# The gated activation of the second feed-forward: formed with tokens on the partitions, and only the product transposed

## What is computed

```python
D_FF_2 = -(-8 * D_MODEL // (3 * 256)) * 256
h = rmsnorm(x, norm_ffn[layer])
a, b = jnp.split(h @ w_ffn_in[layer], 2, axis=-1)
x = x + ((jax.nn.silu(a) * b) @ w_ffn_out[layer]).astype(x.dtype)
```

## Time and profile before

| | |
|---|---|
| three executions | 868.4, 869.7, 872.04 us |
| the profiled execution, its own time | 871.05 us |
| its span, first to last instruction | 868.8 us |
| mean granted clock of TensorE | 0.969 of full speed |
| TensorE matmuls, busy | 797.1 us (92%), 3811 instructions |
| VectorE, busy | 550.6 us (63%) |
| ScalarE, busy | 485.9 us (56%) |
| GpSimd, busy | 86.6 us (10%) |
| weights and inputs read | 128.6 MB, 149 GB/s over the span |
| second feed-forward, wide groups and down groups | from 686 to 865 us |

### The profile page before, as it was taken

How to read it: one execution, slowest core, us unless ns; L and a number is a source line. 1 busy time by engine, 2 the same in 40 slices (tenths; PEclk the granted TensorE clock), 3 DMA queues, 4 the chain that set the end, 5 groups by cost and what they waited for, 6 DMA issues and landing times.

```text
span 868.8 us, 10702 instructions
## 1 busy us (share of the span) xinstructions
PE 797.1 (92%) x3811; PEld 647.7 (75%) x3811; DVE 550.6 (63%) x817; ACT 485.9 (56%) x743; POOL 86.6 (10%) x50
## 2 busy tenths in 40 slices
PE   4989999999799999999999798796859999999998
PEld 3777788777588888888887577663637888888886
DVE  5676676567556777776463477687673666665650
ACT  4755656666236777774264744342543677776630
POOL 0023000000000000000000056644231000000000
PEclk9989999999999999999999899798969999999999
DMA  8766333344237655456383533221001675554550
GB/s 303 292 203 198 103 116 119 97 147 140 68 120 251 211 193 193 151 170 204 105 270 124 179 98 97 78 68 49 25 25 48 215 237 182 177 184 173 191 165 24
DMA packets 70566, 130.21 MB, mean 150 GB/s; under 512 B 5534, under 2 KB 17142, under 8 KB 70142
## 3 DMA queue, kind: packets, MB, share of 16 engines
q1 hardware_dynamic: 69662, 124.90, 44.2%
q10 hardware_dynamic: 864, 4.78, 1.5%
HBM read 128.61 MB, written 1.05 MB: 149 GB/s over the span
## 4 chain that ended last, share of the span: by engine, by line
PE 74%; DVE 11%; ACT 7%; DMA 4%; issue 2%; POOL 1%; SPq 1%; ACTq 0%; DVEq 0%; POOLq 0%
PE acc L478 20%; PE acc L480 20%; PE acc L479 20%; DMA b_raw<-in_w_in 2%; DVE b_wlo L1186 2%; PE banks L579 2%; PE banks L704 2%; PE banks L539 2%; PE banks L564 2%; PE banks L717 1%; DMA b_raw<-in_w_mem_kv 1%; ACT b_whi L825 1%; PE banks L552 1%; PE banks L543 1%; PE banks L566 1%
## 5 line engine op out<-in xcount | busy, mean ns | idle before, releaser
L1186 DVE TENSOR_TENSOR b_wlo<-b_raw,b_whi 128x1024 fp32r<-128x1024 f32 (+4 forms) x222 | 253.1, 1179 | 102.8 <-ACT b_whi L825 101.4
L825 ACT ACTIVATE b_whi<-b_raw 128x1024 fp32r<-128x1024 f32 (+4 forms) x244 | 234.3, 1001 | 77.1 <-DMA b_raw<-in_w_in 19.3
L478 PE MATMUL acc<-b_whi,b_hhi 128*128 128x512 f32 (+4 forms) x528 | 205.0, 388 | 10.3 <-DVE b_hlo L1459 4.6
L479 PE MATMUL acc<-b_whi,b_hlo 128*128 128x512 f32 (+4 forms) x528 | 198.2, 375 | 0.0
L480 PE MATMUL acc<-b_wlo,b_hhi 128*128 128x512 f32 (+4 forms) x528 | 197.8, 375 | 0.0
L478 PEld LDWEIGHTS acc<-b_whi,b_hhi 128*128 128x128 f32 x528 | 100.9, 191 | 31.0 <-DVE b_hlo L1459 5.1
L480 PEld LDWEIGHTS acc<-b_wlo,b_hhi 128*128 128x128 f32 x528 | 100.8, 191 | 15.8
L479 PEld LDWEIGHTS acc<-b_whi,b_hlo 128*128 128x128 f32 x528 | 100.8, 191 | 15.8 <-issue 1.5
L478 PE MATMUL acc<-b_whi,b_ohi 128*128 128x512 f32 (+1 forms) x272 | 105.8, 389 | 5.4 <-DVE b_wlo L1186 2.9
L480 PE MATMUL acc<-b_wlo,b_ohi 128*128 128x512 f32 (+1 forms) x272 | 103.4, 380 | 0.0
L479 PE MATMUL acc<-b_whi,b_olo 128*128 128x512 f32 (+1 forms) x272 | 103.1, 379 | 0.0
(11 more groups left out here) (214 smaller groups left out, 909.0 us busy)
## 6 DMA issues: line engine op xcount, KB each, us to landing
b_raw<-in_w_in SPq DMA_DIRECT2D x48, 512.0 KB, 4.8
b_raw<-in_w_ffn_up SPq DMA_DIRECT2D x40, 512.0 KB, 4.8
b_raw<-in_w_ffn_in SPq DMA_DIRECT2D x40, 512.0 KB, 4.7
b_raw<-in_w_ffn_down SPq DMA_DIRECT2D x22, 512.0 KB, 6.0
b_raw<-in_w_ffn_out SPq DMA_DIRECT2D x22, 512.0 KB, 4.7
b_raw<-in_w_out SPq DMA_DIRECT2D x16, 512.0 KB, 3.7
b_raw<-in_w_in SPq DMA_DIRECT2D x12, 412.0 KB, 3.6
b_raw<-in_w_in SPq DMA_DIRECT2D x8, 410.0 KB, 3.5
```

The costliest lines, as they stand in the source:

```text
L478: nc.tensor.matmul(o, a, wh, start=first, stop=False)
L479: nc.tensor.matmul(o, b, wh, start=False, stop=False)
L825: A(whi[:, n % SPLIT, 0:c["nk"], 0:c["n"]], raw[:, n % RAW, 0:c["nk"], 0:c["n"]], ACT.Copy)\
L1186: V.tensor_tensor(wlo[:, n % SPLIT, 0:c["nk"], 0:c["n"]], raw[:, n % RAW, 0:c["nk"], 0:c["n"]], whi[:, n % SPLIT, 0:c["nk"], 0:c["n"]].bit ...
```

## The change

The feed-forward of the second block gets functions of its own, `ffn2`, on TensorE, ScalarE and VectorE; `ffn1` is the old code for the first. In `ffn2` the sums of the gate half are read twice by ScalarE (scaled Copy to `gtok`, scaled Abs to `ltok`); Exp, Ln, the logarithm, Exp and the weighing y * sigmoid follow with tokens on the partitions. VectorE then reads the sums of the up half, multiplies by the token's norm factor and by the weighed gate and writes `utok`. TensorE transposes `utok` alone (banks 0 and 1), ScalarE writes the high part straight from the bank and VectorE the low part. `etok` and `ltok` are other views of the buffers `e` and `lg`.

```diff
+        etok, ltok = [b.rearrange("p c t -> p (c t)").rearrange("p (t n) -> p t n", t=T) for b in (e, lg)]
...
+            def act_T(i=0, short=""):
+                for t in range(T):
+                    pe.wait_ge(*moved(f"u2{short or '_0'}", t, i))
+                for b in range(1 if short else 2):
+                    claim(b, f"a2{short}T", i)
+                    for c in range(2):
+                        for t in range(T):
+                            mm = nc.tensor.transpose(X[b][:, c * S + t * P:c * S + (t + 1) * P],
+                                                     utok[:, t, (2 * b + c) * P:(2 * b + c + 1) * P], ident)
+                    full(mm, b, f"a2{short}T", i)
+
+            def ffn2():
+                after_norm("ffn2", "g2s", "u2s")
+                gemm("g2_0", 0)
+                gemm("g2_0", 1)
+                act_T(short="s")
+
+                with pe.Fori(0, PAIRS - 1) as i:
+                    cnt.enter()
+                    gemm("u2_0", 0, i)
+                    gemm("u2_0", 1, i)
+                    gemm("g2_0", 0, i + 1)
+                    act_T(i)
+                    gemm("g2_0", 1, i + 1)
+                cnt.leave(PAIRS - 1)
+                gemm("u2_0", 0, PAIRS - 1)
+                gemm("u2_0", 1, PAIRS - 1)
+                for c in range(-(-FT // (CK * PART))):
+                    if c < PAIRS:
+                        pe.wait_ge(*at("bank1 free", "a2T", c))
+                    gemm("d2_0", c)
+                    if c == 0:
+                        act_T(PAIRS - 1)
+                gemm("d2_1")
...
+                def gate_in(i=0, short=""):
+                    name, n = f"g2{short or '_0'}", REST if short else CN
+                    if not short:
+                        v = cnt.value("gate weighted", "2", i) - 1
+                        act.wait_ge(sem("gate weighted"), v if known else 1)
+                    for t in range(T):
+                        a = sums(act, name, t, i)
+                        scaled(gtok[:, t, 0:n], a[:, 0:n], ACT.Copy, "ffn2", t)
+                        leave(scaled(ltok[:, t, 0:n], a[:, 0:n], ACT.Abs, "ffn2", t), name, t, i)
...
+                hi_to(first + PART - 1)
+                gate_in(short="s")
+                hi_to(first + 2 * PART - 1)
+                gate_log(short="s")
+                hi_to(first + 3 * PART - 1)
+                sigmoid(short="s")
+                hi_to(first + 4 * PART - 1)
+                act_hi(short="s")
+                with act.Fori(0, PAIRS) as i:
+                    cnt.enter()
+                    gate_in(i)
+                    for n in range(PER, PER + PART):
+                        hi_one(first + n, i)
+                    gate_log(i)
+                    for n in range(PER + PART, PER + 2 * PART):
+                        hi_one(first + n, i)
+                    sigmoid(i)
+                    for n in range(PER + 2 * PART, 2 * PER):
+                        hi_one(first + n, i)
+                    act_hi(i)
...
+                def product(i=0, short=""):
+                    name, n = f"u2{short or '_0'}", REST if short else CN
+                    dve.wait_ge(*at("gate weighted", f"2{short}", i))
...
+                    for t in range(T):
+                        a = sums(dve, name, t, i)
+                        leave(V.scalar_tensor_tensor(utok[:, t, 0:n], a[:, 0:n], rs[:, rstd("ffn2", t)],
+                                                     etok[:, t, 0:n], ALU.mult, ALU.mult), name, t, i)
...
+                with dve.Fori(0, PAIRS) as i:
+                    cnt.enter()
+                    for n in range(PER, PER + PART):
+                        lo_one(first + n, i)
+                    gate_log(i)
+                    for n in range(PER + PART, PER + 2 * PART):
+                        lo_one(first + n, i)
+                    weigh(i)
+                    for n in range(PER + 2 * PART, 2 * PER):
+                        lo_one(first + n, i)
+                    product(i)
+                    act_lo(i)
```

More of the change, by code:

```diff
@@ L946, in gate_in @@
                         blk = FT - 2 if short else 4 * i + 2 * b
[L947 to L955, removed]
+                        for c in range(2):
+                            ins = A(y[:, 2 * b + c, :], X[b][:, c * S:(c + 1) * S], ACT.Identity,
+                                    bias=vT[:, bass.ds(blk + c + 3 * FT, 1)],
+                                    scale=vT[:, bass.ds(blk + c + 2 * FT, 1)])
+                        done(ins, "gate in", f"{m}{short} {b}", i)
                 def finish(i=0, short=""):
@@ L991, in ffn, with ffn2, gate_log, sigmoid @@
                 hi_to(groups[f"d{m}_0"]["last"] + 2 * PART)
[L992 to L995, removed]
+                norm("x2", "d1_1", hhi, None, "norm_ffn_2")
+            def ffn2():
+                first = groups["g2_0"]["first"]
+                def gate_in(i=0, short=""):
[7 more added lines that the diff above has]
+                        leave(scaled(ltok[:, t, 0:n], a[:, 0:n], ACT.Abs, "ffn2", t), name, t, i)
+                def gate_log(i=0, short=""):
+                    n = REST if short else CN
+                    act.wait_ge(*moved(f"g2{short or '_0'}", 1, i))
+                    done(A(ltok[:, :, 0:n], ltok[:, :, 0:n], ACT.Exp, scale=-1.0), "gate exp", f"2{short}", i)
+                    act.wait_ge(*at("gate exp", f"2{short}", i))
+                    done(A(ltok[:, :, 0:n], ltok[:, :, 0:n], ACT.Ln, bias=1.0), "gate ln", f"2{short}", i)
+                def sigmoid(i=0, short=""):
+                    n = REST if short else CN
+                    act.wait_ge(*at("gate log", f"2{short}", i))
+                    done(A(etok[:, :, 0:n], etok[:, :, 0:n], ACT.Exp), "gate sigmoid", f"2{short}", i)
+                def act_hi(i=0, short=""):
+                    for b in range(1 if short else 2):
+                        act.wait_ge(*at(f"bank{b} full", f"a2{short}T", i))
+                        dst = ahi[:, FT - 2:FT, :] if short else ahi[:, bass.ds(4 * i + 2 * b, 2), :]
+                        done(A(dst, X[b].rearrange("p (c t) -> p c t", t=S), ACT.Copy), "act hi", f"2{short} {b}", i)
+                hi_to(first + PART - 1)
[18 more added lines that the diff above has]
+                    act_hi(i)
+                cnt.leave(PAIRS)
+                nxt[0] = first + PER + PER * PAIRS
+                hi_to(groups["d2_1"]["last"])
@@ L1311, in pv_low, with ffn1 @@
                      "bank3 free", f"pv {j}")
-            def ffn(m):
+            def ffn1():
+                m = 1
                 first = groups[f"g{m}_0"]["first"]
@@ L1355, in ffn @@
                 lo_to(first + 2 * PART - 1)
-                if m == 1:
-                    conv(short="s")
+                conv(short="s")
                 lo_to(first + 4 * PART - 1)
@@ L1370, in ffn, with ffn2, gate_log, weigh @@
                 nxt[0] = first + PER + PER * PAIRS
[L1371 to L1376, removed]
+                norm("x2", "d1_0", "d1_1", hhi, hlo, gain_at(3))
+            def ffn2():
+                first = groups["g2_0"]["first"]
+                def gate_log(i=0, short=""):
+                    n = REST if short else CN
+                    dve.wait_ge(*at("gate ln", f"2{short}", i))
+                    done(V.scalar_tensor_tensor(etok[:, :, 0:n], gtok[:, :, 0:n], 0.0, ltok[:, :, 0:n], ALU.min,
+                                                ALU.subtract), "gate log", f"2{short}", i)
+                def weigh(i=0, short=""):
+                    n = REST if short else CN
+                    dve.wait_ge(*at("gate sigmoid", f"2{short}", i))
+                    done(V.tensor_tensor(etok[:, :, 0:n], gtok[:, :, 0:n], etok[:, :, 0:n], ALU.mult), "gate weighted",
+                         f"2{short}", i)
+                def product(i=0, short=""):
+                    name, n = f"u2{short or '_0'}", REST if short else CN
+                    dve.wait_ge(*at("gate weighted", f"2{short}", i))
+                    if not short:
+                        for b in range(2):
+                            v = cnt.value(f"bank{b} full", "a2T", i) - 1
+                            dve.wait_ge(sem(f"bank{b} full"), v if known else 1)
+                    for t in range(T):
+                        a = sums(dve, name, t, i)
+                        leave(V.scalar_tensor_tensor(utok[:, t, 0:n], a[:, 0:n], rs[:, rstd("ffn2", t)],
+                                                     etok[:, t, 0:n], ALU.mult, ALU.mult), name, t, i)
+                def act_lo(i=0, short=""):
+                    for b in range(1 if short else 2):
+                        dve.wait_ge(*at("act hi", f"2{short} {b}", i))
+                        blks = slice(FT - 2, FT) if short else bass.ds(4 * i + 2 * b, 2)
+                        done(V.tensor_tensor(alo[:, blks, :], X[b].rearrange("p (c t) -> p c t", t=S),
+                                             ahi[:, blks, :].bitcast(F32), ALU.subtract), f"bank{b} free",
```

(15 more changed lines are left out.)

55 lines of the change are left out of this document (26 added, 29 removed).

## The result

The changed kernel took 875.59 us (median of 19 executions) against 869.96 for the kernel before on the same chips: a ratio of 1.0067, 95% interval 1.0050 to 1.0084, or some 5.8 us. The profiled execution has a span of 874.4 us against 868.8, 5.6 us more, and all of it lies in the second feed-forward: from the last wait ahead of it (680.66 us after, 680.70 before) to the last addition on VectorE (870.87 after, 865.34 before) it is 190.21 us against 184.64.

The account below looks back on a forecast made before the run. TensorE, busy throughout the second feed-forward, was taken as the bound: -4.79 - 0.14 + 4 x 1.14 + 2.7 = +2.3 us, so 872.0 us against 869.7, range 867.0 to 876.5.

Parts of the forecast that it names:

- Saving on TensorE: Second feed-forward: 44 of 88 transposes go, saving 4.79 us, plus 0.14 us for one group that had waited.
- The engines' sums: Per pair ScalarE has some 2 us less work, VectorE the same within 0.2 us; neither becomes the bound.
- The walk through a pair: Queue order per pair: up chunk 3 lands late, so TensorE waits 1.0 us ahead of the product's transposes; 1.14 with restart.
- Restart: Extra time of a transpose group on TensorE that had to wait: 0.14 us (1.01 against 0.87).
- The short pair: Wait ahead of the short pair's product transposes on TensorE: taken as 0, bounds 0 and 1.1 us.
- The first pair: Pair 0: ScalarE reads the gate sums late, behind the short product's high part; 1.6 us more, 2.7 us in all.
- The clock: TensorE's granted clock after pair 0's wait: no fall assumed; 2.6 us at half clock would cost 1.3 us.
- the full gain: Rival: queues keep up and nothing waits on TensorE; -4.9 us, 864.8 us, chance 0.07.
- The late transfer: Rival: up chunk 3 of each pair lands beyond 4.8 us; at 5.4 us +5.3 us, 875.0 us; chance 0.22.
- slower: Outcome of a loss above the measurable bound of 0.5%, 4.35 us; chance 0.22.

Follow-up runs that it names:

- product one low part earlier: Changed kernel with VectorE's product ahead of the last up chunk's low part, behind three of four; ratio 0.9974 to the kernel before.
- gate sums first: Changed kernel with ScalarE reading pair 0's gate sums ahead of the short pair's high part; ratio 1.0026 to the kernel before.
- idle transposes: Changed kernel with eight extra identity transposes per pair on TensorE just ahead of the product's transposes; ratio 1.0047 to the kernel before.
- log later: Changed kernel with Exp, Ln and log behind all four gate chunks, sigmoid and weighing behind two up chunks; ratio 0.9985 to the kernel before.
- half transfers: Changed kernel whose transfers of up chunks 2 and 3 (down chunks in the last pair) bring 128 of 256 rows; ratio 0.9954 to the kernel before.
- product two and one low parts earlier: Two runs: changed kernel with VectorE's product behind two, or three, of the four up chunks' low parts; ratios 0.9951 and 0.9974 to the kernel before.
- both edits: Changed kernel with the product behind two of four up low parts and ScalarE reading pair 0's gate sums earlier; ratio 0.9952 to the kernel before.

## Why the prediction came out as it did

I forecast 872.0 us, 2.3 more than the kernel before, and the time is 5.6 to 5.8 more; it lies in the range, on the far side of the half per cent for which I gave 0.22. The mechanism was right, sizes were off: +5.6 in the stretch where the sum says +2.3.

- **Saving on TensorE, 4.79 + 0.14 us:** right. With the waits gone the ratio is 0.9951, 4.3 us, interval 2.1 to 6.5; the stretch is 4.84 us shorter, and the profile shows pairs of 22.65 us where the sum says 22.71.
- **The engines' sums:** right. VectorE's work is the same within 1 us over the stage, ScalarE's 13 us less (I said some 2 us a pair).
- **The walk through a pair:** right in every link that it has; it left out the transfer of up chunk 2, which lies 0.3 us behind in pairs 1 and 2. The wait stands where it said. It gave 1.0 us; measured 1.05, 1.31, 1.16 and 0.93, and landings of up chunk 3 of 4.6 to 4.8 us for the 4.8 taken. Restart: 0.16 to 0.23 for the 0.14 taken. That is 0.7 us more over the four pairs.
- **The short pair, 0 us:** 0.26, and 0.15 for the restart.
- **The first pair, 2.7 us:** 3.06 and a restart of 0.16, 0.5 more. The transfer of up chunk 3 took 5.0 us there and not 4.8; the delay from the order on ScalarE was as worked out (its reading starts at 698.28, walked 698.0).
- **The clock, taken as 0:** this is the term that was mis-sized. I had its price, 1.3 us, and named the place, but chose "no fall" since one of two gaps of like length showed none. The same trace has more such gaps: after 2.08 us ahead of 42.97 and 2.89 us ahead of 15.29 the mean clock over the next 2.6 us was 0.55 and 0.62, and after 3.63 us ahead of 591.04 it was 1.00: falls were at least as frequent (rows in the last section). It fell and cost 1.6 us in the profiled execution. That is half of what is missing; the waits and restarts above are the other half. Whether it falls varies from one execution to the next (last section), so a term of about half the price was the best to be had, and a part of how near the forecast came is luck.
- **Rivals:** the full gain was not there, but the experiments show how it is had. The rule of the Trainium skill (page "Perfetto Trace Analysis", section "Identifying the Most-Contended Engine") that the most-contended engine is to be optimized first holds for 0.9951 and not for 1.0067: both take the same work from TensorE. The late transfer as a rival was priced from landings of 5.2 us on; the landings were not that late. Without the 1.6 us of the clock the loss would be some 4.0 us, so it took the clock to bring it over 0.5%.

I also weighed "slower" too lightly in another way: the sum stood at +2.3 with every neglected effect on the same side. A wait brings a restart (0.15 to 0.23 us here) and may bring a slower clock, and neither is a gain.

## What to carry to other kernels

Taking work from the engine that bounds a kernel is worth nothing if what the engine then waits for was moved to a later place in another queue; so walk one period of each queue in order, with the transfers and the buffers that release them. An instruction whose operands are ready should not stand behind one that waits for a transfer: look for the last wait ahead of it in its queue, and try the neighbouring places, which add no instruction. When a wait on TensorE is forecast, add its restart, and for one of about 2 us and more half the price of a slower clock behind it, as long as the traces at hand show it falling about as often as not.

## What the runs showed of the hardware

The granted clock after a wait of TensorE in the middle of dense work, by the waits of this stage: it stayed at 1.00 after 1.34 us (product one low part earlier), 1.33 us (gate sums first, pair 1) and 2.00 us (idle transposes, whose eight transposes of 1.0 us stood just ahead of the wait), and fell to 0.50 after 1.96 us (log later) and to steps of 0.43 us after 3.06 us (changed kernel), while before it stayed at 1.00 after 3.03 us. So the length of the wait alone does not decide.

Nor does the place in the program. The gap of the earlier trace rows at 229.07 stands, with the same code behind it, in all nine traces of this case, 2.98 to 3.03 us long, each time with TensorE busy at 1.00 for the 3 us ahead of it. Over the next 2.6 us the clock was 1.00 in five of them (before, changed, log later, gate sums first, half transfers) and 0.50 in four (product two and one low parts earlier, idle transposes, both edits). The gap of 2.89 us at 15 us, also in all nine, was followed by a slower clock in three. After 1.57 us at 237 us and 1.83 us at 474 us it stayed at 1.00 in all nine; after 1.71 us at 616 us it fell in four (places as in the kernel before). None of the runs tells what decides. Two gaps of the kernel before that were followed by a fall, and the window behind the first:

```profile
42.97 0.60 PE L478 MATMUL acc<-b_whi,b_hhi 128*128 128x512 f32 x1 [2.08 <-DVE b_wlo L1186]
...
43.00:46.00 3.00, 3.00 (x8) 2.34 (x9) 3.00 (x3) 0.64 (x1) 0.00 (x0) 0.54 0.60 167
...
15.29 0.50 PE L478 MATMUL acc<-b_whi,b_ohi 128*128 128x512 f32 x1 [2.89 <-DVE b_wlo L1186]
```

The price was 1.6 us in both falls of this stage, read off the distance of two groups (25.53 us in the changed kernel; with the log later 735.90 - 710.87 - 22.71 - 0.53 - 0.16 = 1.6).

A transfer of 256 KB landed in 2.9 to 3.2 us where one of 512 KB took 4.3 to 5.0, in the same places of the same burst in the first two pairs.
